# Recurrent stage: paired products on four quarters of TensorE, and steps of the next pair in other places

## The reference

```python
def step(S, inp):
    r_t, w_t, k_t, v_t, av_t, bv_t = inp
    sa = jnp.einsum('bhvk,bhk->bhv', S, av_t)
    S = S * w_t[:, :, None, :] + sa[..., None] * bv_t[:, :, None, :] + v_t[..., None] * k_t[:, :, None, :]
    return S, jnp.einsum('bhvk,bhk->bhv', S, r_t)
...
mu = jnp.mean(y, axis=-1, keepdims=True)
var = jnp.mean(jnp.square(y - mu), axis=-1, keepdims=True)
yn = ((y - mu) * lax.rsqrt(var + GN_EPS)).reshape(B, T, W) * lnx_w + lnx_b
out = (yn + bonus.reshape(B, T, W)) * g
```

## Time and profile before

| | us |
|---|---|
| median of 3 runs (2424.48 to 2425.45) | 2424.97 |
| the profiled execution | 2424.27 |
| its span in the profile | 2422.6 |
| TensorE busy in the span | 2375.1 |
| VectorE busy in the span | 1461.7 |
| ScalarE busy in the span | 895.2 |

### The profile page before, as it was taken

One profiled execution on the slowest core, in us unless ns is written; L12 is line 12 of the kernel. 1 busy time (PEld: TensorE's weight loads), 2 busy tenths in 40 slices (PEclk: granted clock), 3 DMA queues, 4 the chain that ended last, 5 costly groups with the idle time before them and its releaser, 6 DMA issues.

```text
span 2422.6 us, 48639 instructions
## 1 busy us (share of the span) xinstructions
PE 2375.1 (98%) x19616; PEld 2272.0 (94%) x19616; DVE 1461.7 (60%) x2052; ACT 895.2 (37%) x1040; POOL 131.4 (5%) x203
## 2 busy tenths in 40 slices
PE   8999999999999999999999998999999999999998
PEld 6899999898988889888999988999999999999998
DVE  5645544555677666776544446666666666666676
ACT  6443344343333333332434344333333333333334
POOL 3000001000000010000000001000000000000003
PEclk9999999999999999999999999999999999999999
DMA  7554487342333333323444632444444444444443
GB/s 267 185 162 145 156 290 244 104 141 83 96 98 95 93 126 100 97 86 95 142 150 151 202 121 89 158 154 139 156 156 140 154 150 144 140 158 153 152 143 110
DMA packets 282189, 346.67 MB, mean 143 GB/s; under 512 B 6957, under 2 KB 240733, under 8 KB 280907
## 3 DMA queue, kind: packets, MB, share of 16 engines
q1 hardware_dynamic: 271883, 307.66, 39.6%
q0 software_dynamic: 9712, 36.30, 4.5%
q10 hardware_dynamic: 464, 0.79, 0.1%
HBM read 333.83 MB, written 10.89 MB: 142 GB/s over the span
## 4 chain that ended last, share of the span: by engine, by line
PE 86%; DVE 8%; issue 3%; ACT 2%; DMA 1%; DVEq 0%; SPq 0%; ACTq 0%
PE bank L246 20%; PE bank L247 20%; PE bank L255 20%; PE bank L1165 5%; PE bank L227 4%; PE bank L228 4%; PE bank L229 4%; DVE work L906 1%; ACT hi L211 1%; DVE lo L218 1%; PE bank L1181 1%; PE bank L511 1%; DVE q L833 1%; PE bank L512 1%; PE bank L518 1%
## 5 line engine op out<-in xcount | busy, mean ns | idle before, releaser
L218 DVE TENSOR_TENSOR lo<-raw,hi 128x2048 fp32r<-128x2048 f32 x286 | 655.6, 2292 | 505.5 <-ACT hi L211 488.0
L246 PE MATMUL bank<-ah,hi 128*128 128x320 f32 x3200 | 958.0, 313 | 0.2 <-DVE al L532 0.2
L247 PE MATMUL bank<-al,hi 128*128 128x320 f32 x3200 | 945.8, 309 | 0.0
L211 ACT ACTIVATE hi<-raw 128x2048 fp32r<-128x2048 f32 x286 | 548.0, 1916 | 924.1 <-PE bank L255 675.4
L246 PEld LDWEIGHTS bank<-ah,hi 128*128 128x128 f32 x3200 | 600.7, 188 | 12.9 <-issue 9.8
L247 PEld LDWEIGHTS bank<-al,hi 128*128 128x128 f32 x3200 | 601.1, 188 | 0.4
L255 PE MATMUL bank<-ah,lo 128*128 128x320 f32 x3200 | 546.6, 311 | 0.0
L255 PEld LDWEIGHTS bank<-ah,lo 128*128 128x128 f32 x3200 | 486.4, 188 | 3.7 <-issue 0.8
L227 PE MATMUL bank<-bh,hi 128*128 128x320 f32 x704 | 218.7, 311 | 0.2 <-DVE work L2314 0.2
L229 PE MATMUL bank<-bh,lo 128*128 128x320 f32 x704 | 217.6, 309 | 0.0
L228 PE MATMUL bank<-bl,hi 128*128 128x320 f32 x704 | 217.5, 309 | 0.0
(11 more groups left out here) (377 smaller groups left out, 2035.7 us busy)
## 6 DMA issues: line engine op xcount, KB each, us to landing
raw<-in_w_in SPq DMA_DIRECT2D x98, 1024.0 KB, 5.3
raw<-in_w_up SPq DMA_DIRECT2D x88, 1024.0 KB, 5.1
raw<-in_w_down SPq DMA_DIRECT2D x44, 1024.0 KB, 5.1
raw<-in_w_branch SPq DMA_DIRECT2D x24, 1024.0 KB, 5.4
raw<-in_w_out SPq DMA_DIRECT2D x16, 1024.0 KB, 5.5
raw<-in_w_mem_k SPq DMA_DIRECT2D x8, 1024.0 KB, 5.5
raw<-in_w_mem_v SPq DMA_DIRECT2D x8, 1024.0 KB, 5.3
work<-in_cache_mem_k POOLq DMA_DIRECT2D x8, 1024.0 KB, 6.0
```

The source lines that it names most:

```text
L211: act.activation(hi[c % NS][:, :], raw[c % 2][:, :], ACT.Copy).then_inc(S("hi_done"), 1)
L218: dve.tensor_tensor(lo[c % NS][:, :], raw[c % 2][:, :], hi[c % NS][:, :], ALU.subtract)\
L246: pe.matmul(out, w, xh[:, 8 * h + k, :], start=h + k == 0, stop=False)
L247: pe.matmul(out, w, xl[:, 8 * h + k, :], start=False, stop=False)
```

## The change

- Chunks 0 and 1 (`TURNED`) now cross over: head 0 goes from rows 0-63 to output partitions 64-127 and head 1 the other way, and their results stay swapped until they are used. Two steps form one group (`both`): the products of the turned and of the upright chunks alternate and go to two banks. A and B become ABt and ABs, beT and Cb beCt and beCs (bank 6), Bk and Ck BCt and BCs, vT and kaT vkt and vks.
- G and the parts of S0 to S3 that don't need the state before become one group, St and Ss; S1 to S3 add what comes from the state before. X is cut into X1 and X. Four products of Y stand between those of S4.
- bonus and ssq stand first in the pair, z and za behind vks. bonus is copied out by ScalarE; its product with v and ScalarE's root for the norm come early; the maximum with 1e-24 becomes a minimum with 1e12 on the inverse.
- On VectorE `prepare_norm` and `prepare_k` move to RT2, `prepare_logs` behind Z1, `branch(0, 1)` and `prepare_kk` behind the copy of y, `weights_low(4)` behind the square for the variance. `STEPS` has other places and numbers. ScalarE takes s0t and alT after z and za.

The core of the diff:

```diff
-        for _n in ["A", "bonus", "B", "beT", "Cb", "A2", "B2", "Bk", "vT", "RT1", "B4", "Ck", "kaT", "RT2", "s0t",
-                   "Q", "QT", "Z0", "Z0s", "Q2", "QT2", "XB", "Z1", "QT4", "alT", "Z2", "z", "za", "ssq", "Z3", "X4", "G",
-                   "S0", "S1", "S2", "S4", "S3", "X", "g", "mean", "trp", "var", "tr0", "tr1"]:
+        for _n in ["bonus", "ssq", "ABt", "ABs", "beCt", "beCs", "A2", "B2", "BCt", "BCs", "RT1", "B4", "vkt", "vks", "z", "za", "RT2", "s0t",
+                   "Q", "QT", "Z0", "Z0s", "Q2", "QT2", "XB", "Z1", "QT4", "alT", "Z2", "Z3", "X4", "St", "Ss",
+                   "S1", "X1", "S2", "S4", "S3", "X", "g", "mean", "trp", "var", "tr0", "tr1"]:
...
+        def prepare_norm(dve, vv, j):
+
+
+            dve.wait_ge(S("kk_root"), j + 1)
+            vv.do(dve.reciprocal(sq, sq))
+            vv.do(dve.scalar_tensor_tensor(out=kkv, in0=sq, scalar=1e12, in1=kkv, op0=ALU.min, op1=ALU.mult))
...
             vv.do(dve.tensor_scalar(tmp, av, -1.0, pcol("k_a", j), ALU.add, ALU.mult))
             vv.do(dve.scalar_tensor_tensor(out=row_(j + 8), in0=tmp, scalar=1.0, in1=row_(j + 8), op0=ALU.add, op1=ALU.mult))
-
-        def prepare_norm(dve, vv, j):
-
-            dve.wait_ge(S("kk_root"), j + 1)
-            vv.do(dve.reciprocal(sq, sq))
-            vv.do(dve.tensor_tensor(kkv, kkv, sq, ALU.mult))
             vv.do(dve.tensor_tensor(av, kkv, av, ALU.mult))
 
...
 
 
-        STEPS = {"A": 8, "A2": 3, "RT1": 3, "RT2": 3, "Q": 3, "XB": 3, "Z2": 4, "Z3": 4, "S0": 2, "S1": 2, "S2": 2, "S3": 1, "X": 2,
+        STEPS = {"bonus": 8, "A2": 3, "RT1": 3, "RT2": 3, "Q": 3, "XB": 3, "alT": 4, "Z3": 3, "St": 1, "S1": 3, "S2": 3, "S3": 3,
                  "g": 5, "mean": 2, "var": 1}
-        Y_STEPS = 3
+        HELD = {"alT": 4, "g": 3}
         STEPS = {PR[_n]: v for _n, v in STEPS.items()}
...
+                    m = m[:, chunks[0]:chunks[0] + k, :] if len(m.shape) == 3 else bmid(m[:, :], k)
+                    tt(c5(o)[:, chunks[0]:chunks[0] + k], c3(pbank(name)[:, at:at + 64 * k]), m, ALU.mult, sem)
+
+                for name, cs in (("ABt", TURNED), ("ABs", UPRIGHT)):
+                    k, states = 64 * len(cs), tuple(c for c in cs if c < NCK)
+                    ps(name)
+                    part(t_ad, name, 0, cs, m_ad)
+                    part(t_bd, name, k, cs, m_bd)
+                    part(t_bo, name, k, states, m_bo, "ring_out")
+                for name, cs in (("beCt", TURNED), ("beCs", UPRIGHT)):
+                    k = 64 * len(cs)
+                    ps(name)
+                    vv.do(dve.tensor_copy(zc3[:, cs[0]:cs[-1] + 1, 0:64], c3(pbank(name)[:, 0:k])))
+                    tt(zc3[:, cs[0]:cs[-1] + 1, 64:128], c3(pbank(name)[:, k:2 * k]), m_in[:, cs[0]:cs[-1] + 1, :], ALU.mult, "ring_out")
...
                 plain(t_bd, "B4")
-                masked(t_ck, "Ck", m_in)
+                dve.wait_ge(S("turned_out"), OUT0_A + N_OUT_A * i + OUT_A["bonus"] + 1)
+                tt(bon, bon, row_(i + 16), ALU.mult)
+                prepare_norm(dve, vv, i + 1)
                 plus(t_rt, "RT2")
-                prepare_kk(dve, vv, i + 1)
+                prepare_k(dve, vv, i + 1)
                 plain(t_a2, "Q", TP)
                 plain(t_b2, "QT", TP)
...
+                prepare_logs(dve, vv, i + 1)
                 plain(t_rt, "QT4", TP)
                 plus(zc, "Z2", 512)
                 weights_low(2)
-                ps("ssq")
-                vv.do(dve.tensor_scalar(sq, pbank("ssq")[:, 0:T], 1e-24, None, ALU.max), "ring_out")
                 plus(zc, "Z3", 512)
-                prepare_logs(dve, vv, i + 1)
                 ps("X4")
                 tt(t_x[:, TP:T], t_x[:, TP:T], pbank("X4")[:, 0:64], ALU.add, "ring_out")
-                ps("G")
-                tt(c3(step_), c3(pbank("G")[:, 0:192]), bmid(m_id[:, :], NCK - 1), ALU.add, "ring_out")
+                ps("St")
+                tt(c3(st_all[:, 0:128]), c3(pbank("St")[:, 0:128]), bc(pend_p[:, 0:2], CH), ALU.mult)
+                tt(step_[:, 0:64], pbank("St")[:, 128:192], m_id[:, :], ALU.add, "ring_out")
+                ps("Ss")
+                tt(c3(st_all[:, 128:256]), c3(pbank("Ss")[:, 0:128]), bc(pend_p[:, 2:4], CH), ALU.mult)
+                tt(c3(step_[:, 64:192]), c3(pbank("Ss")[:, 128:256]), bmid(m_id[:, :], 2), ALU.add, "ring_out")
                 dve.wait_ge(S("turned_out"), OUT0_A + N_OUT_A * i + OUT_A["s0t"] + 1)
                 tt(sam, bmid(t_x[:, TP:T], NB), bc(m_e8[:, :], HD), ALU.mult)
                 tt(vtm, bmid(v_t[:, TP:T], NB), bc(m_e8[:, :], HD), ALU.mult, "sam_ready")
 
                 def state(c):
                     ps(f"S{c}")
-                    vv.do(dve.tensor_scalar(st_[c], pbank(f"S{c}")[:, 0:64], pend_p[:, c:c + 1], None, ALU.mult), "ring_out")
-
-                state(0)
-                prepare_k(dve, vv, i + 1)
+                    vv.do(dve.scalar_tensor_tensor(out=st_[c], in0=pbank(f"S{c}")[:, 0:64], scalar=pend_p[:, c:c + 1],
+                                                   in1=st_[c], op0=ALU.mult, op1=ALU.add), "ring_out")
+
                 state(1)
+                ps("X1")
+                tt(t_x[:, 64:128], t_x[:, 64:128], pbank("X1")[:, 0:64], ALU.add, "ring_out")
+                state(2)
                 branch(0, 0)
-                state(2)
                 weights_low(3)
                 ps("S4")
                 tt(sam, pbank("S4")[:, :].rearrange("p (b v) -> p b v", b=NB), s0t, ALU.add)
                 tt(sam, sam, bc(pend_s, HD), ALU.mult, "ring_out")
                 state(3)
-                branch(0, 1)
                 ps("X")
-                tt(t_x[:, 64:TP], t_x[:, 64:TP], pbank("X")[:, 0:192], ALU.add, "ring_out")
-                prepare_norm(dve, vv, i + 1)
-                weights_low(4)
+                tt(t_x[:, 128:TP], t_x[:, 128:TP], pbank("X")[:, 0:128], ALU.add, "ring_out")
                 prepare_al(dve, vv, i + 1)
                 dve.wait_ge(S("y_ps"), i + 1)
                 vv.do(dve.tensor_copy(y_, bank[6][:, 0:T]), "y_out")
+                branch(0, 1)
                 prepare_rest(dve, vv, i + 1)
+                prepare_kk(dve, vv, i + 2)
                 branch(1, 0)
                 ps("g")
                 vv.do(dve.scalar_tensor_tensor(out=bon, in0=bon, scalar=pcol("lnx_b", i), in1=bank[6][:, 0:T],
...
                 vv.do(dve.scalar_tensor_tensor(out=ym, in0=pbank("mean")[:, 0:T], scalar=-1.0 / HD, in1=y_,
                                                op0=ALU.mult, op1=ALU.add), "ring_out")
                 tt(ysq, ym, ym, ALU.mult, "ym_sq")
+                weights_low(4)
...
                 i = j - 1
-                for name, dst, n in (("vT", v_t, T), ("kaT", ka_t, T), ("s0t", qr[:, 896:1408], 512), ("alT", alp_t, 192)):
+                ps("bonus")
+                act.wait_ge(S("gated_out"), j)
+                aa.do(act.activation(bon, pbank("bonus")[:, 0:T], ACT.Copy), "turned_out")
+                act.wait_ge(S("wkv_ps"), PS0 + NPR * i + PR["ssq"] + 1)
+                aa.do(act.activation(sq, pbank("ssq")[:, 0:T], ACT.Sqrt), "kk_root")
+                for name, c, k in (("vkt", 0, 128), ("vks", 128, 192)):
                     ps(name)
-                    aa.do(act.activation(dst[:, 0:n], pbank(name)[:, 0:n], ACT.Copy), "turned_out")
+                    o = pbank(name)
+                    aa.do(act.activation(v_t[:, c:c + k], o[:, 0:k], ACT.Copy))
+                    aa.do(act.activation(ka_t[:, c:c + k], o[:, k:2 * k], ACT.Copy), "turned_out")
                 ps("z")
             else:
...
+                aa.do(act.activation(qr[:, 896:1408], pbank("s0t")[:, :], ACT.Copy), "turned_out")
+                ps("alT")
+                aa.do(act.activation(alp_t[:, 0:192], pbank("alT")[:, 0:192], ACT.Copy), "turned_out")
             act.wait_ge(S("logs"), j + 1)
             aa.do(act.activation(pt, cum, ACT.Exp), "exps")
...
+                def into_chunk(o, a, b, c):
+                    for h in range(2):
+                        last = pe.matmul(o[half(h ^ (c in TURNED)), :], a[half(h), :], b[half(h), :], start=True, stop=True)
+                    return last
+                def out_of_chunk(o, a, b, c, start=True, stop=True, **kw):
+                    for h in range(2):
+                        r = half(h ^ (c in TURNED))
+                        last = pe.matmul(o[half(h), :], a[r, :], b[r, :], start=start, stop=stop, **kw)
+                    return last
+                def both(turned, upright, a1, b1, a2, b2):
...
+
+                    t, s = begin(turned), begin(upright, ahead=1)
+                    if turned == "ABt":
+                        wait("ops_ready", i + 1)
...
+                    one(t, a1, b1, 0, 0)
+                    one(s, a1, b1, 3, 1)
+                    one(t, a1, b1, 1, 1)
+                    one(s, a1, b1, 4, 2)
+                    one(t, a2, b2, 0, 2)
+                    one(s, a2, b2, 2, 3)
+                    end(one(t, a2, b2, 1, 3))
```

(24 more changed lines are left out.)

180 lines of the change are left out of this document (98 added, 82 removed).

## The result

| | before | after |
|---|---|---|
| median, 13 runs each (us) | 2424.51 | 2430.30 (2426.85 to 2432.55) |
| ratio after to before, 95% interval | | 1.0023 (1.0015 to 1.0032) |
| profiled execution, its span (us) | 2424.27, 2422.6 | 2426.85, 2424.8 |
| mean granted clock of TensorE | 0.997 | 0.995 (the other twelve: 0.992 to 0.995) |

The change makes the kernel slower by 0.23%, 5.8 us, where I forecast no change. Note two things from the start: the profiled execution is the fastest of the 13, 3.4 us under the median, and the clock is not the same on both sides.

The account below looks back on a forecast made before the run. TensorE, busy 597 of 607 us, was taken to bound the stage. Its 5.6 us saved per pair return as waits: 9.95 + 8.9 + 57.45 = 76.3 us against 76.31, so 2424 us, range 2414 to 2432.

Parts of the forecast that it names:

- at the full clock: Reading of the changed stage before the change: TensorE busy 597 of 607 us, VectorE 405, with the clock at full.
- The 5.6 us saved on TensorE are given back: Per pair: 1.8 us returns as waits in the pair, the rest as waits for VectorE and behind trp.
- The loop of a pair: y's copy to trp's copy 9.95, on to A/B 8.9, to the next y's copy 57.45: 76.3 us, against 76.31 before.
- Waits 1 to 4: New TensorE waits ahead of BCs 0.5, vks 0.3, at za 0.4, ahead of St 0.6 us; bounds together 0.5 to 3.
- TensorE's work: From A to the end of the Y stretch, 5.6 us less a pair; y's copy possible after 55.7 instead of 61.26.
- the groups': Four paired groups (A with B and so on) go from 10 chunk times to 6 each: 1.87 us less a pair.
- 0.58 us for twenty records: Price of small TensorE products read from the earlier trace, giving 0.117 us for one chunk (two heads, two passes).
- The wait ahead of var: TensorE's wait for ym_sq from VectorE, before trp's copy: some 0.7 us.
- The one ahead of tr1: TensorE finishes tr0 some 2 us before VectorE's copy of trp, delayed by weight split 4, and waits for it.
- More waits of the same kind: Slower rival: beC waits for ssq's square root on ScalarE; bounds leave 0.6 us a pair more, 2429 us; chance 12 in 100.
- What would make it wrong: Refuting signs: no gap at tr1, quarters' records spaced 0.058 us one behind another, or A/B starting with gated_out, not bonus.
- The signs I listed: Group of 20 + 20 records in 0.75 us, pair near 76.3, tr1 gap about 2, St wait, late hi split, VectorE idle.

Follow-up runs that it names:

- split_ahead_al: The changed kernel with weight split 4 back at its old place on VectorE, ahead of prepare_al; 2410.20 us, ratio to before 0.9942.
- fill_var: The changed kernel with five extra identity products a pair on TensorE, only in the wait ahead of var; 2425.06 us, ratio to before 1.0004.
- fill_tr: The changed kernel with five extra identity products a pair on TensorE, only ahead of tr0's transposes; 2424.94 us, ratio to before 1.0000.
- before_split_behind_sq: The kernel before with only weight split 4 moved behind the square for the variance on VectorE; 2437.67 us, ratio to before 1.0055.
- split_behind_trp: The changed kernel with weight split 4 one place later on VectorE, behind the copy of trp; 2424.35 us, ratio to before 0.9997.
- w_both5: The changed kernel with ten extra identity products a pair, five ahead of var and five ahead of tr0's transposes; 2423.33 us, ratio to before 0.9995.

## Why the prediction was wrong

**The step that failed** stands in "What bounds the kernel now": "at the full clock". I read 1.00 in a kernel whose TensorE waits little, and carried it into one for which I had just worked out several microseconds of waits a pair. Every term of the sum was priced at the full clock, and none of the rivals had another. The runs showed 1.4 us for each pair with a low stretch, three in the traced run; the changed kernel with its two waits filled takes 2423.33 us, against 2424 forecast and 2430.3 measured without the filling. "The 5.6 us saved on TensorE are given back" was only half of it: the waits that they turned into have a price of their own.

Point by point:
- *The loop of a pair*: 9.95 + 8.9 + 57.45 = 76.3 was forecast, 9.90 + 9.07 + 57.22 = 76.19 measured. Right, and for the reason given: split_ahead_al took the split out of it and the pair fell by 1.6 us.
- *Waits 1 to 4*: 1.8 us forecast, about 1.2 measured: 0.1 ahead of BCs for 0.5, 0.2 ahead of vks for 0.3, 0.3 to 0.4 at za for 0.4, 0.5 ahead of St for 0.6. *TensorE's work*: 5.6 less forecast; 61.26 + 1.2 - 57.22 leaves 5.2. The mis-sized term is the groups', 0.3 us each instead of 0.47. By that alone 4.9 would be left, so the other terms together gave some 0.3 more than I put down; which of them, no run shows. Waits and work are off by about 0.6 and 0.4, one against the other: that 57.22 comes so close to 57.45 is in part luck. (0.58 us for twenty records was a slip, too: the earlier trace rows give 1.80 / 3 = 0.60, so 0.12 a chunk. It moves the sum by less than 0.1.)
- *The wait ahead of var*: 0.7 forecast, 1.3 measured. The one ahead of tr1: about 2 forecast, 1.4 measured. The first made no difference to the loop, but it ends 1.2 us ahead of the second, and the two together bring the lower clock.
- *No rival* was the right one. "More waits of the same kind" would have ended at 2429, close to 2430, by a mechanism that the trace doesn't show: the undisturbed pairs are shorter than before, not longer.
- *What would make it wrong* named a missing gap at tr1, records in turn, and A/B behind gated_out. None of them came. The signs I listed appeared, some in another size (a group took 0.84 us for 0.75, the gap at tr1 1.4 for 2; VectorE waits 2.6 us for the hi split at lo split 2), and the time was another; they tested the chain and never the clock.

What stays open: why one pair gets the low stretch and the next, with the same two waits, does not. The traced run has them in pairs 1, 3 and 7. That in the stage it takes both waits rests on five kernels (one wait each in fill_var, fill_tr, split_ahead_al, before_split_behind_sq; both but further apart in split_behind_trp) with one traced run each; their medians agree with it. And the number of low stretches in the other twelve runs of the changed kernel is an estimate.

Elsewhere it doesn't take two waits. At about 472 us, ahead of the stage, TensorE waits once for 1.9 us in all fourteen traces, with no other wait of size in the ten microseconds before. In eight of them, such as fill_tr, the clock then falls:

```profile
471.34 0.44 PE L1762 MATMUL bank<-ident,small 128*128 128x128 f32 x2 [1.89 <-DVE small L1647]
470.00:480.00 10.00, 8.49 (x48) 8.12 (x48) 6.02 (x13) 3.21 (x4) 4.36 (x1) 0.83 0.31 101
```

In the other six, the kernels before and after the change and w_both5 among them, the same wait leaves 1.00 in that row. So the unevenness isn't particular to the stage, and 1.9 us in one piece can be enough where 1.3 or 1.4 wasn't.

## What to carry to other kernels

When a change saves work on TensorE but leaves the loop closed by another engine, the saving becomes idle time on TensorE, and here that was not free: look where the new waits fall and whether two of them stand close together, and compare the clock in windows of ten microseconds, since 0.995 against 0.997 over the whole run already stands for the 4 us of three low stretches here. A filler of useless products inside the waits is a cheap test for this: a kernel that gets faster by doing more, as w_both5 did, points at the clock. And when a chain is relieved of one item, ask at once what closes the loop next: taking the split back gave 1.6 us of 2.45, and it took the branch sum, prepare_kk and ScalarE's hi split to bring the rest.
